# A hybrid decoder block on one core: token tile 0 projected alone, attended and normalised inside the projection stage, its expert selection started at the fourth attention item

## The reference, cut to what matters

```python
proj = x @ w_in                                  # (1024, 1024) @ (1024, 3080)
q, k, v, z, xbc, dt_raw = split(proj)            # q, k, v, z: 512 columns each, xbc: 1024
q, k = apply_rope(q), apply_rope(k)
att = diff_attention(q, k, v, lam)               # causal, 4 heads x 2 components, blocks of 128 queries
ssd = ssd_mixer(z, xbc, dt_raw, ...)             # conv + silu, chunked scan over 8 chunks, gate with silu(z), norm
mix = concat([att, ssd]) @ w_out                 # (1024, 1024) @ (1024, 1024)
x = layer_norm(alpha * x + mix, ln1_g, ln1_b)
# PEER feed-forward: 8 heads, each picks 16 of 16384 experts by product keys, gathers rows of u and v
ffn = peer_ffn(x, peer_wq, peer_keys, peer_u, peer_v)
x = layer_norm(alpha * x + ffn, ln2_g, ln2_b)
```

## Time and profile before

| | |
|---|---|
| three runs | 3304.97, 3316.07, 3319.42 us; median 3316.07 us |
| span of the profiled execution, first to last instruction | 3313.3 us |
| its own time | the page gives none beside the span; the median of the runs is 2.8 us above the span |
| busy: TensorE, VectorE, GpSimd, ScalarE | 2784.6, 1887.9, 1483.6, 596.6 us |
| mean granted TensorE clock | 0.918 of full speed |
| moved by DMA | 981.57 MB, 296 GB/s over the span |

### The profile page before, as it was taken

The page is one execution under the profiler, slowest core; times in us unless marked ns, Lnnn a source line. Parts: engine busy times, 40 slices in busy tenths (PEclk is TensorE's granted clock), DMA queues, the critical chain, the costliest instruction groups (busy, mean ns, idle before and its releaser), DMA issues.

```text
span 3313.3 us, 32683 instructions
## 1 busy us (share of the span) xinstructions
PE 2784.6 (84%) x10171; PEld 1374.6 (41%) x10171; DVE 1887.9 (57%) x4634; ACT 596.6 (18%) x1288; POOL 1483.6 (45%) x1348
## 2 busy tenths in 40 slices
PE   8999979755356888757589999999999999899996
PEld 3455545433123555424334444444444444344442
DVE  3335444688698888678845655546666544444113
ACT  1321033321004888500000000000000000000000
POOL 0011001345644443344565666566665566565452
PEclk9999979877677899878799999999999999999998
DMA  3100021355877999898999999999999999999995
GB/s 119 39 26 26 26 74 67 128 188 208 290 275 277 387 385 387 320 358 314 328 395 387 397 404 405 368 403 401 404 404 376 364 398 407 387 398 384 369 372 204
DMA packets 307579, 981.57 MB, mean 296 GB/s; under 512 B 29904, under 2 KB 57680, under 8 KB 306640
## 3 DMA queue, kind: packets, MB, share of 16 engines
q0 software_dynamic: 184320, 671.17, 53.1%
q1 hardware_dynamic: 120464, 307.85, 24.7%
q10 hardware_dynamic: 2624, 0.46, 0.1%
HBM read 941.63 MB, written 37.75 MB: 296 GB/s over the span
## 4 chain that ended last, share of the span: by engine, by line
PE 30%; issue 13%; POOL 11%; DMA 10%; DVE 6%; ACT 2%; ACTq 1%; DVEq 1%; POOLq 0%
PE part L1806 10%; PE hid L1787 9%; DMA v_ring<-in_peer_v_dram,ids_t 8%; POOL u_ring L1725 7%; PE acc L1844 6%; POOL v_ring L1739 4%; PE turn_ps L1779 4%; DVE u_ring L2122 2%; DMA u_ring<-in_peer_u_dram,ids_u 1%; ACT dense_sums L1884 1%; PE part L1815 1%; ACTq L1885 1%; ACT dense_sums L1886 1%; DMA room<-in_peer_v_dram 1%; DVE dense_sums L2130 1%
## 5 line engine op out<-in xcount | busy, mean ns | idle before, releaser
L2122 DVE CUSTOM_DVE_ANT_0 u_ring<-u_ring,x_rows_in 128x1024 f32<-128x1024 f32 x560 | 676.7, 1225 | 510.0 <-DMA u_ring<-in_peer_u_dram,ids_u 497.3
L1725 POOL DMA_INDIRECT u_ring<-in_peer_u_dram,ids_u x560 | 628.4, 1122 | 501.7 <-DVE dots L2122 357.7
L1739 POOL DMA_INDIRECT v_ring<-in_peer_v_dram,ids_t x560 | 593.7, 1060 | 479.2 <-PE acc L1844 334.0
L1806 PE MATMUL part<-room 128*128 128x512 f32 x1536 | 693.2, 601 | 88.5 <-DVE room L2098 76.4
L1787 PE MATMUL hid<-x1t_dense,room 128*128 128x384 f32 x2048 | 699.9, 495 | 6.3 <-DMA room<-in_peer_ut_dram 4.8
L1787 PEld LDWEIGHTS hid<-x1t_dense,room 128*128 128x128 f32 x2048 | 385.7, 193 | 340.3 <-issue 101.0
L1806 PEld LDWEIGHTS part<-room 128*128 128x128 f32 x1536 | 292.1, 192 | 448.2 <-issue 338.0
L1844 PE MATMUL acc<-v_ring,line 128*32 128x512 f32 x2240 | 292.6, 643 | 67.7 <-DMA v_ring<-in_peer_v_dram,ids_t 65.4
L1922 ACT ACTIVATE room<-hid 128x384 f32<-128x384 f32 x128 | 62.9, 491 | 1465.8 <-PE hid L1787 1465.8
L2108 DVE TENSOR_TENSOR dense_sums<-dense_sums,part 128x512 f32<-128x512 f32 x186 | 125.9, 685 | 270.9 <-PE part L1806 270.7
L412 PE MATMUL bank<-w_ring,xt 128*128 128x512 f32 x512 | 225.1, 592 | 2.7 <-issue 2.7
(11 more groups left out here) (320 smaller groups left out, 2640.9 us busy)
## 6 DMA issues: line engine op xcount, KB each, us to landing
wq_pair<-in_peer_wq_dram SPq DMA_DIRECT2D x32, 2048.0 KB, 14.6
room<-in_peer_ut_dram SPq DMA_DIRECT2D x128, 512.0 KB, 7.4
room<-in_peer_v_dram SPq DMA_DIRECT2D x128, 512.0 KB, 9.8
gate_grid<-room SPq DMA_DIRECT2D x6, 4096.0 KB, 14.0
room<-gate_grid SPq DMA_DIRECT2D x32, 768.0 KB, 18.4
w_ring<-in_w_in_dram SPq DMA_DIRECT2D x5, 2048.0 KB, 8.0
u_ring<-in_peer_u_dram,ids_u POOLq DMA_INDIRECT x560, 9.7
v_ring<-in_peer_v_dram,ids_t POOLq DMA_INDIRECT x560, 10.4
```

The source lines that it names most:

```text
L1725: pool.indirect_dma_start(u_ring[:, n % U_RING, :], None, peer_u, bass.IndirectOffsetOnAxis(ap=ids_u[:, q, k:k + 1], axis=0))\
L1739: pool.indirect_dma_start(row, None, peer_v, bass.IndirectOffsetOnAxis(ap=ids_t[:, q % 2, token:token + 1], axis=0))\
L1806: last = mm.matmul(part[k % 3][:], weights[:, n % 2, i, d * P:(d + 1) * P], vd[:, slot, half * 512:(half + 1) * 512], start=(i == 0), stop ...
L2122: vec.tensor_tensor_reduce(u_ring[:, n % U_RING, :], u_ring[:, n % U_RING, :], x1[:, q % 2, :], 1.0, 0.0, ALU.mult, ALU.add, dots[:, q % 2 ...
```

## The change

1. **Tile 0 is projected ahead, alone.** `blocks` gets a list of tiles for each entry: after the two xbc blocks come k, q, z and v for tile 0 only, then z for tiles 1 to 7, v for tiles 1 to 3, two output-projection groups of tile 0 ("o", the halves of `w_out`), v for tiles 4 to 7, and k and q for tiles 1 to 7. There are 13 block loads instead of 6, and 34 steps instead of 32.
2. **Tile 0's attention, output projection and normalisation** are placed at fixed steps of this stage (`first_tile`), on all engines, with XT as their PSUM bank. Its three vectors and its rows of x are loaded at the start of the stage; its results are stored from the same stage.
3. **The attention stage drops tile 0**: `ORDER = (1, 7, 6, 5, 4, 3, 2)`, 28 items, 40 steps. `CHOICE = 3`, and `FIRST_SLOTS` is 112. The sync queue loads x for the first two tiles and the weights of the later pairs ahead of the loop over tiles.
4. **The expert stage** has 16 rows of u of tile 0 left (2 steps instead of 6), and the v rows of tile 0 start at step 2 instead of 6.
5. Several buffers are moved into others (`wq_pair`, `q_t`, `k_t` are lent in the projection stage).

```diff
-FIRST_SLOTS = 5 * TOPK
+FIRST_SLOTS = 7 * TOPK
...
-        blocks = [("xbc", 2048), ("xbc", 2560), ("z", 1536), ("v", 1024), ("k", 512), ("q", 0)]
-        steps = 4 * NT
+        rest = tuple(range(1, NT))
+        blocks = [("xbc", 2048, range(8)), ("xbc", 2560, range(8)), ("k", 512, (0,)), ("q", 0, (0,)), ("z", 1536, (0,)), ("v", 1024, (0,)),
+                  ("z", 1536, rest), ("v", 1024, rest[0:3]), ("o", 0, (0,)), ("o", 512, (1,)), ("v", 1024, rest[3:]),
+                  ("k", 512, rest), ("q", 0, rest)]
+        after = [(kind, t) for kind, _, tiles in blocks[2:] for t in tiles]
+        steps = len(after)
+        turns = [t for t in after if t[0] in "kq"]
+        SCORE_AT, TURN_P_AT, WEIGH_AT, TURN_Z_AT, TURN_ATT_AT, TURN_X1_AT = (3, 5), 8, 9, 11, 12, (17, 18)
...
+                    if n == 1:
+                        sp.dma_start(x1_first[:], x[0:P, :]).then_inc(x0_in, 16)
+                        for dst, src in ((g1_first, ln1_g), (b1_first, ln1_b), (sub_g_first, subln_g)):
+                            sp.dma_start(dst, src.partition_broadcast(P)).then_inc(affine_in, 16)
+                sp.wait_ge(first_normed, 1).then_inc(first_normed, -1)
+                sp.dma_start(x1_dram[0:P, :], x1_first[:]).then_inc(first_stored, 16)
+                sp.wait_ge(first_turned, 2).then_inc(first_turned, -2)
+                sp.dma_start(x1t_dram[0:P, :], x1t_first[:].rearrange("p c n -> p (c n)")).then_inc(first_stored, 16)
...
+                def first_scores(c):
+                    pe.wait_ge(xt_free, 1).then_inc(xt_free, -1)
+                    for h in range(DA_HEADS):
+                        rows = slice(c * DA_DIM, (c + 1) * DA_DIM)
+                        at = slice(h * P, (h + 1) * P)
+                        mm.matmul(XT[:, at], q0_t[rows, h, :], k_t[rows, h, 0:P], start=True, stop=False)
+                        last = mm.matmul(XT[:, at], ident[:], mask_qk[:], start=False, stop=True)
+                    last.then_inc(first_scored, 1)
+                def first_tile(s):
+                    if s in SCORE_AT:
+                        first_scores(SCORE_AT.index(s))
+                    if s == TURN_P_AT:
+                        pe.wait_ge(first_w, 1).then_inc(first_w, -1)
+                        pe.wait_ge(xt_free, 1).then_inc(xt_free, -1)
+                        for h in range(DA_HEADS):
+                            last = mm.transpose(XT[:, h * P:(h + 1) * P], p0_first[:, h, :], ident[:])
+                        last.then_inc(xt_done, 1)
...
-        ORDER = (0, 1, 7, 6, 5, 4, 3, 2)
+        ORDER = (1, 7, 6, 5, 4, 3, 2)
+        last_tile = len(ORDER) - 1
+        items = len(ORDER) * DA_HEADS
...
-        CHOICE = 15
+        CHOICE = 3
...
                 load_pair(0)
+                for t in range(2):
+                    load_rows(t)
+                for g in range(1, HEADS // 2):
+                    sp.wait_ge(wq_free, 1).then_inc(wq_free, -1)
+                    load_pair(g)
...
-U_COUNTS = (6 * (8,), 9 * (8,) + 8 * (7,), 29 * (4,) + 4 * (3,), 29 * (4,) + 4 * (3,), 29 * (4,) + 4 * (3,))
-U_BASE = (0, 48, 176, 304, 432)
+U_COUNTS = (2 * (8,), 9 * (8,) + 8 * (7,), 29 * (4,) + 4 * (3,), 29 * (4,) + 4 * (3,), 29 * (4,) + 4 * (3,))
+U_BASE = (0, 16, 144, 272, 400)
-V_AT = (6, 34, 67, 100, 133)
+V_AT = (2, 34, 67, 100, 133)
```

More of the change, by code:

```diff
@@ L176, in build_mixer @@
         freq = sb("freq", [P, HALF], to=scan)
-        ang = sb("ang", [P, NT, HALF], to=scan)
-        whole = sb("whole", [P, NT, HALF], to=scan)
         trig = sb("trig", [P, 2, NT, HALF], to=scan)
@@ L381, in _ @@
                 group = 0
-                for n, (kind, _) in enumerate(blocks):
+                for n, (kind, _, tiles) in enumerate(blocks):
                     slot = n % 2
@@ L385, in _ @@
                         pe.wait_ge(w_landed[slot], 16).then_inc(w_landed[slot], -16)
-                    for i in range(8):
+                    for i in tiles:
                         s = group - 2 * NT
@@ new lines, in _ @@
+                    if s == SCORE_AT[1] + 1:
+                        dve.wait_ge(first_probs, 2).then_inc(first_probs, -2)
+                        vec.reciprocal(rinv_first[:], rsum_first[:])
+                        dve.drain()
+                        vec.scalar_tensor_tensor(out=ratio_first[:], in0=rinv_first[:, :, 1], scalar=minus_lam[:, 0:1],
+                                                 in1=rsum_first[:, :, 0], op0=ALU.mult, op1=ALU.mult)
+                        dve.drain()
+                        for h in range(DA_HEADS):
+                            vec.scalar_tensor_tensor(out=p0_first[:, h, :], in0=p1_first[:, h, :], scalar=ratio_first[:, h:h + 1],
+                                                     in1=p0_first[:, h, :], op0=ALU.mult, op1=ALU.add)
+                        dve.drain().then_inc(first_w, 1)
@@ new lines, in _ @@
+                    if s == WEIGH_AT + 1:
+                        dve.wait_ge(first_att, 1).then_inc(first_att, -1)
+                        vec.tensor_scalar(av_first[:], av_first[:], 1.0 / DA_V, RMS_EPS, ALU.mult, ALU.add)
+                        dve.drain().then_inc(first_av, 1)
+                    if s == WEIGH_AT + 2:
+                        dve.wait_ge(affine_in, 48).then_inc(affine_in, -48)
+                        vec.tensor_scalar(sub_g_first, sub_g_first, 1.0 - LAMBDA_INIT, None, ALU.mult)
+                        dve.drain()
+                        dve.wait_ge(first_ar, 1).then_inc(first_ar, -1)
+                        for h in range(DA_HEADS):
+                            vec.scalar_tensor_tensor(out=att_first[:, h, :], in0=att_first[:, h, :], scalar=ar_first[:, h:h + 1], in1=sub_g_first,
+                                                     op0=ALU.mult, op1=ALU.mult)
+                        dve.drain().then_inc(first_att_scaled, 1)
@@ new lines, in _ @@
+                    if kind == "o":
+                        half = x1_first[:, t * 512:(t + 1) * 512]
+                        if t == 0:
+                            dve.wait_ge(x0_in, 16).then_inc(x0_in, -16)
+                        dve.wait_ge(dve_group, 1).then_inc(dve_group, -1)
+                        vec.scalar_tensor_tensor(out=half, in0=half, scalar=ALPHA, in1=bank[s % 2][:], op0=ALU.mult, op1=ALU.add)
+                        dve.drain().then_inc(bank_free[s % 2], 1)
+                        vec.bn_stats(stats_first[:, t, :], half)
+                        if t:
+                            dve.drain()
+                            vec.bn_aggr(mv_first[:], stats_first[:].rearrange("p a b -> p (a b)"))
+                            dve.drain()
+                            vec.tensor_scalar(var_first[:], mv_first[:, 1:2], LN_EPS, None, ALU.add)
+                            dve.drain().then_inc(first_var, 1)
@@ new lines, in _ @@
+                    if s and after[s - 1] == ("o", 1):
+                        dve.wait_ge(first_rstd, 1).then_inc(first_rstd, -1)
+                        vec.tensor_scalar(x1_first[:], x1_first[:], mv_first[:, 0:1], rstd_first[:, 0:1], ALU.subtract, ALU.mult)
+                        dve.drain()
+                        vec.tensor_tensor(x1_first[:], x1_first[:], g1_first, ALU.mult)
+                        dve.drain()
+                        vec.tensor_tensor(x1_first[:], x1_first[:], b1_first, ALU.add)
+                        dve.drain().then_inc(first_normed, 1)
+                        dve.sem_inc(first_normed, 2)
@@ L783, in build_mixer @@
         op_free = sem("op_free")
-        xtile_in = sem("xtile_in")
+        xtile_in = [sem(f"xtile_in{i}") for i in range(2)]
         var_ready = handshake("var_ready1")
@@ L856, in tail @@
             t, rest = divmod(n - lag, DA_HEADS)
-            return t if rest == 0 and 0 <= t < NT else None
+            return t if rest == 0 and 0 <= t <= last_tile else None
         with nc.Block() as block:
@@ L913, in _ @@
                         pool.sem_inc(x1_turn, 1)
-                        if t == 0:
-                            pool.tensor_copy(x1_first[:], tile).then_inc(x1_first_ready, 1)
                     for k in rows_asked(n):
@@ L1011, in _ @@
                             for c in range(KC):
-                                last = mm.matmul(out[:], mix_t[:, c, :], w_ring[:, half, c, :],
+                                last = mm.matmul(out[:], mix_t[:, c, :], w_ring[:, 1 - half, c, :],
                                                  start=(c == 0), stop=(c == KC - 1))
@@ L1086, in _ @@
                         act_.activation(sc_pair[:], OP[:], ACT.Copy)
-                        act.drain().then_inc(pair_for_pe, 1)
+                        act.drain().then_inc(pair_for_pe if tail(n + 1, 10) is not None else op_free, 1)
                         act.sem_inc(pair_for_dve, 2)
```

215 lines of the change are left out of this document (161 added, 54 removed).

## The result

The kernel after takes 3354.77 us (median of 4 runs, 3351.33 to 3364.96); the kernel before, on the same chip, 3312.19 (3304.97 to 3319.42). The ratio is 1.0132, interval [1.0105, 1.0159]: 43 us slower where 12.5 were forecast, and outside the forecast's range of 3288 to 3350.

What follows compares the result with a forecast made beforehand. Bounds: projection TensorE; attention a chain, no full engine; expert steps 2 to 5 the query-weight loop, 7 to 12 DMA. 28.9 + 2.1 - 18.5 = +12.5 us: span 3325.8, plus 2.8, 3329; range 3288 to 3350.

Steps and rivals of the forecast that it cites:

- the attention stage's sum: Attention stage, tile by tile from analogous rows: +2.1 us; bounds -17 if all added products hide, +20 if none does.
- The tiles that take over choice and products: Attention tiles 6, 5 and 4, priced by earlier tiles doing the same work: 66.5, 68.6 and 68 us.
- Tile 3 ... no longer waits for `pair_for_pe`: 61: Attention tile 3 keeps choice and products, but its output projection loses a wait: 61 us, -5.3.
- Tile 2 "51.5": Attention tile 2 loses two heads of choice, 9.4 us each, and gets 2.5 back: 51.5 us, -16.3.
- the tails lose two heads too ... 84.5: Attention tails lose two heads; 3 us come back through GpSimd's gathers and the last projection: 84.5 us, -15.7.
- Tile 7 "42.5": Attention tile 7 loses tile 0's output projection (-10 us) and gains query product 2: 42.5 us for 45.5, -3.
- The sum puts about 17 of them on the path: Attention stage: of 36.8 us for 32 more VectorE products, about 17 lengthen the stage.
- sentence on slowed products: Attention stage: products meet GpSimd's multiplications in six tiles instead of four, two slowed products each: 8.5 us of harm.
- Projection: Projection stage: +28.9 us, from 20.4 of added TensorE work (scores and masks 3.5) and 8.5 of load stalls.
- Expert stage: Expert stage: -18.5 us, from steps 2 to 5 (-2), step 6 (-6) and token steps 13 to 16 (-10.5).
- the fast rival: Idle time takes all added attention products, and expert steps 2 to 5 take 18.3 us: 3290 in all, chance 0.2.
- The slower rival: Early v rows starve the query weights, so expert steps 2 to 5 take 31 us: 3359 in all, chance 0.12.

Runs made afterwards that it cites:

- experiment 3: Kernel after with the second output-projection bank given from index 3 on (`t >= 3`) instead of 4: 3351.1 us, 1.0106 of the kernel before.
- Experiment 1: Kernel before with only tile 0 moved into the projection stage, choice at its old place, 80 rows in attention: 3323.4 us, 1.0022 of the kernel before.
- experiment 2: Experiment 1 with the early choice (`CHOICE = 3`) added, still 80 rows in the attention stage: 3342.6 us, 1.0098 of the kernel before.
- experiments 8 and 9: Gain and bias moved from GpSimd to VectorE: 8 in the kernel after, 3336.9 us (1.0072); 9 in the kernel before, 3312.7 us (1.0009).
- experiment 12: Kernel after with each of the 112 attention-stage products cut to 128 of 1024 columns: 3298.1 us, 0.9959 of the kernel before.
- Experiment 5: Kernel after with the v rows of tile 0 back at step 6 of the expert stage: 3353.0 us, 1.0122 of the kernel before.

## Why the prediction was wrong

**The step that failed is the attention stage's sum**: "+2.1" measured as +21.9, 2 us past the upper bound that the prediction named ("+20 if none does"), though not for that bound's reason. What was mis-sized is above all its late part, the time that tiles 3 and 2 and the tails were to give back: 37.3 forecast, 14.6 measured. By its terms:

- *The tiles that take over choice and products* (6, 5, 4): forecast by their analogs, 5.4 us too low in 203. Right. Tile 1: 1.2 too low.
- *"Tile 3 ... no longer waits for `pair_for_pe`: 61"*: 69.3. The index in `second_bank` moved with `ORDER`; the bank brings 6.0 of the 8.3 back (experiment 3).
- *Tile 2 "51.5" and "the tails lose two heads too ... 84.5"*: together 14.4 us longer. The prediction took the whole work of the heads that leave as path; 17.6 us came off for 31.3 of VectorE, and of the heads' work alone 0.67 (experiments 1 and 2). In the last tail the chain goes through GpSimd's in-order queue: gathers hold up gain, bias and the scale of `att`, and its passes slow VectorE's. Taking gain and bias off GpSimd returns 12 of the 14.4 in the kernel after and nothing in the kernel before (experiments 8 and 9). This edit removes both effects at once, so how the 12 divide between late start and slow operation is open.
- *Tile 7 "42.5"*: 33.0, the one term priced too high, by 9.5. Experiment 1, without a query product there, has 28.8 for 45.5: the output projection and norm of tile 0 were worth 16.7, not 10, and the query product adds 4.7 (experiment 2), not 7. The other terms are too low by 29.3 together, so this one, by luck, hides a third of the miss.
- *"The sum puts about 17 of them on the path"* (its own bounds, 37 us apart, put it at 19): the 32 rows alone lengthened the stage by 22.2, from experiment 2 to the kernel after. Nearly right as a number, by luck as a picture. All 32 came to stand in tile 2 and the tails (64 instructions of VectorE more, 150.4 us for 124.4), where by experiment 12 the time of the products themselves is worth only 0.26 of 36.8, 10 us. No run divides the other 16; GpSimd, which issues the gathers, is busy 89 us in this stretch for 47.

What was not seen as one thing is that the early choice by itself costs 27 us of this stage for the same instructions (experiments 1 and 2), with nothing in the expert stage for it. The prediction booked it tile by tile against the tails, and the give-backs from tile 3 on came out smaller. Its sentence on slowed products (8.5 us, for four more of them) is close: VectorE is 8.7 us busier in experiment 2 than in 1. But only three more are slowed, ten for seven, 6.4 us; most of the rest is the scale of `att`, 5.33 for 3.20 in the last tile. The Trainium skill ("SBUF — State Buffer", section on who interferes with whom) speaks of instructions with two SBUF inputs, not of products alone, and the trace agrees: the scale of `att`, which also has two, took 5.19 us for 1.14.

**Projection, +34.8 for +28.9**: the mechanism is right, stalls 8.3 for 8.5. Mis-sized: scores and masks (6.5 for 3.5, 3.0 low) and the group at a granted clock of 0.80 (1.7), together 4.7 of the 5.9; what makes up the remainder is open. The idle engines did cover the added work: the one wait of TensorE at `XT`, 2.45 us at the last turn of q, stands in the kernel before as well.

**Expert stage, -16.1 for -18.5**: right in sum. Steps 2 to 5 gained nothing (+1.2 for -2). Experiment 5 shows a loop of 16.5 to 18.6 us once the gathers are gone, and it is the gathers that hold it at 24: the fast rival's 18.3 was a fair price for the loop, but not beside gathers. The slower rival came only in single steps (27.9 and 26.6 us in steps 2 and 5, with query weights that landed up to 19.3 us after they were asked for); the mean of 24.1 is far from its 31. Step 6 is right (-5.8 for -6); the token steps gave 6.2 for 10.5; steps 0 and 1 gave 5 that nobody had booked.

**From span to median**: the 2.8 us that the prediction added was three runs' chance: with a fourth run the median before is 3312.2, below its span of 3313.3.

**As a balance by design** (ratios): 7 us for the move, 25 for the early choice, 11 for the rows. The rows give 15.4 us in the expert stage and take 22.2 in attention. The move pays back 27 of 35.

## What to carry to other kernels

When work is moved out of a list that the kernel indexes, search for every threshold on that index: one `t >= 4` cost 6 us here. Work brought forward into a stage whose engines are each 65% busy is not free, and what leaves a later part doesn't come back whole: moving the choice added 0.69 us for each microsecond of VectorE in the early tiles and returned 0.67 at the end. The share can be measured by shortening the instruction, but part by part (0.81 in the tiles and 0.26 in the tails here), and it leaves out what comes with the instruction, such as its gather. And an engine whose queue also issues gathers should not hold a step of the critical chain: two passes a tile taken off GpSimd gave 17 us in the kernel with early gathers, and nothing in the one without.

## What the runs showed of the hardware

- Four scales of 128x128 on VectorE, two SBUF inputs: 1.14 us with no 1024-wide pass of GpSimd beside them, 5.19 beside two (2.33 and 2.43), 3.20 beside the second alone. A product of 1.22 takes 3.35 beside such a pass; with the passes on VectorE none does.
- After two stalls of TensorE (2.24 and 2.27 us, 11 us apart) a group of 16 matmuls took 8.73 us for 7.03 at a granted clock of 0.80; without the stalls it took 7.03, and so did the group after stalls of 1.82 and 1.95.
- A product with 64 rows by 128 columns and the mask's with 128 by 128 take the same time, 0.41 us from start to start.
- The query-weight loop beside no gathers: 16.5 to 18.6 us a step; beside v gathers 19.5 to 27.9, at 374 GB/s.
